# Attention with the two maps of a differential head merged into one output product, the values stationary and the probabilities moving

## The reference, cut to what matters

```python
def mix_groups(dq, dk, dv, gq, gk, gv, lam, lam_init, subln_g):
    sc = HEAD_DIM ** -0.5
    o1 = attend(dq[:, :, :, 0], dk[:, :, :, 0], dv, sc)      # 4 differential heads, map 1, values 128 wide
    o2 = attend(dq[:, :, :, 1], dk[:, :, :, 1], dv, sc)      # map 2, the same values
    o_diff = rmsnorm(o1 - lam.astype(o2.dtype) * o2, subln_g) * (1.0 - lam_init)
    o_gqa = attend(gq, gk, gv, sc)                           # 8 query heads, 2 key/value heads, values 64 wide
    return jnp.concatenate([o_diff.reshape(b, L, -1), o_gqa.reshape(b, L, -1)], axis=-1)
```

## Time and profile before

| what | value |
|---|---|
| median of 3 runs | 2672.94 us (2671.48 to 2678.66) |
| the profiled execution, first to last instruction | 2675.0 us, inside the range of the runs, 2.1 us above their median |
| TensorE busy | 2410.9 us, 90% |
| VectorE busy | 1675.5 us, 63% |
| ScalarE busy | 974.4 us, 36% |
| GpSimd busy | 591.1 us, 22% |
| attention: first DMA issue to VectorE's last operation | 469.8 to 1127.0 us |
| granted TensorE clock, mean | 0.956 of 2.4 GHz |

### The profile page before, as it was taken

One profiled execution on the slowest core, in us unless ns is written; L12 is line 12 of the kernel. 1 busy time (PEld: TensorE's weight loads), 2 busy tenths in 40 slices (PEclk: granted clock), 3 DMA queues, 4 the chain that ended last, 5 costly groups with the idle time before them and its releaser, 6 DMA issues. The chain is left out here.

```text
span 2675.0 us, 44908 instructions
## 1 busy us (share of the span) xinstructions
PE 2410.9 (90%) x11570; PEld 1565.9 (59%) x11571; DVE 1675.5 (63%) x3837; ACT 974.4 (36%) x1958; POOL 591.1 (22%) x393
## 2 busy tenths in 40 slices
PE   7699997699999999869993999999999999999993
PEld 2255553588999888734442555555555555555552
DVE  1213332577776777624444777777788787878886
ACT  0011111465666556511110334333333333333333
POOL 0000000300000000000001244444444344344444
PEclk9899998799999999989996999999999999999997
DMA  9701112500000000051103899878999967779955
GB/s 337 272 29 34 33 25 72 132 25 16 16 24 16 24 24 16 26 184 63 63 31 113 288 302 338 236 207 238 323 344 352 344 158 224 232 195 326 291 141 165
DMA packets 242105, 419.64 MB, mean 157 GB/s; under 512 B 11151, under 2 KB 181391, under 8 KB 241047
## 3 DMA queue, kind: packets, MB, share of 16 engines
q1 hardware_dynamic: 202048, 285.51, 31.1%
q0 software_dynamic: 33984, 123.75, 18.2%
q10 hardware_dynamic: 6044, 10.06, 1.0%
HBM read 338.88 MB, written 80.40 MB: 157 GB/s over the span
## 5 line engine op out<-in xcount | busy, mean ns | idle before, releaser
L1512 PE MATMUL ps_gu<-w_gate_up,gatheredT 128*128 x1680 | 747.8, 598 | 6.8 <-SPq L1320 6.8
L1512 PEld LDWEIGHTS ps_gu<-w_gate_up,gatheredT 128*128 128x128 f32 x1680 | 311.7, 190 | 365.4 <-issue 362.7
L1335 POOL DMA_INDIRECT gathered<-h_scratch,e_gather_index x107 | 303.0, 2832 | 65.8 <-issue 38.3
L1347 POOL DMA_INDIRECT y_scratch<-e_y,e_target_index x104 | 165.5, 1592 | 653.3 <-DVE e_y L1465 617.2
L828 PE MATMUL ps_out<-values,probsT 128*128 128x128 f32 (+1 forms) x2560 | 303.8, 274 | 0.0
L741 DVE TENSOR_REDUCE chunk_max<-ps_scores 128x1 f32<-128x512 f32 (+1 forms) x387 | 222.5, 599 | 126.5 <-PE ps_scores L813 109.2
L828 PEld LDWEIGHTS ps_out<-values,probsT 128*128 128x128 f32 x2560 | 296.7, 192 | 0.5
L1448 DVE TENSOR_TENSOR w_down_low<-w_down,w_down_high 128x2048 fp32r<-128x2048 f32 x105 | 240.7, 2292 | 81.6 <-issue 81.6
L529 PE MATMUL ps_chunk<-w_in_sb,hT 128*128 128x512 f32 (+1 forms) x736 | 286.0, 550 | 1.5 <-ACT hT L339 1.5
L704 ACT ACTIVATE probs<-ps_scores,neg_max 128x512 f32<-128x512 f32 (+1 forms) x387 | 233.7, 613 | 48.5 <-DVE neg_max L746 42.7
L1373 ACT ACTIVATE e_gate_a<-ps_gu 128x256 f32<-128x256 f32 x105 | 40.3, 384 | 543.1 <-PE ps_gu L1512 543.1
(11 more groups left out here) (229 smaller groups left out, 3067.2 us busy)
## 6 DMA issues: line engine op xcount, KB each, us to landing
w_gate_up<-in_w_exp_gate SPq DMA_DIRECT2D x64, 1024.0 KB
w_gate_up<-in_w_exp_up SPq DMA_DIRECT2D x64, 1024.0 KB
w_down<-in_w_exp_down SPq DMA_DIRECT2D x64, 1024.0 KB
w_mod_ring<-in_w_mod SPq DMA_DIRECT2D x24, 1024.0 KB, 11.6
w_in_sb<-in_w_in SPq DMA_DIRECT2D x8, 1152.0 KB, 12.6
q_twice<-qT_scratch SPq DMA_DIRECT2D x34, 256.0 KB, 4.0
x_tile<-in_tokens SPq DMA_DIRECT2D x10, 512.0 KB, 3.4
qT_scratch<-qT_stage SPq DMA_DIRECT2D x20, 256.0 KB, 3.6
```

The costliest lines, as they stand in the source:

```text
L1335: pool.indirect_dma_start(xg[u][:], None, h2_d, bass.IndirectOffsetOnAxis(ap=ti[u][:, 0:1], axis=0), bounds_check=SEQ - 1).then_inc(s_gath ...
L1347: pool.indirect_dma_start(y_d, bass.IndirectOffsetOnAxis(ap=si[u][:, 0:1], axis=0), yb[u][:], None, bounds_check=SEQ + P - 1, compute_op=A ...
L1512: last = nc.tensor.matmul(psG[:], hT[:, k], wgu[:, ds(q & (WS - 1), 1), k].rearrange("p o n -> p (o n)"), start=(k == 0), stop=(k == KD - 1))
```

## The change

Attention is written out anew, with no hardware loop. The work is cut into 24 units. A `d` unit is four query tiles (512 queries) of one differential head; there are 8, in two groups of four. A `g` unit is one query tile and the four query heads of one key/value head; there are 16, in two groups of eight. The order is 4 d, 8 g, 4 d, 8 g.

- Scores: one step makes two maps for 128 queries side by side in five PSUM banks (2560 columns; the third bank holds the end of the first and the start of the second): both maps of a differential head, or two query heads. A d unit has 4 steps, a g unit 2. Now the keys hold high and low in the two halves of one tile, and q is stationary as `qh` and then `ql`. Each is still two fp32r products. There is one set of score banks. The second map's columns in the last bank pair wait for both exponentials of the step before.
- Maxima: one reduce of 1280 columns, one of 256, one of 1024, and a minimum of two. Exponentials: two instructions of 1280 columns.
- Merge, d units only: VectorE makes minus lambda times the quotient of the two row sums; GpSimd multiplies the second map by it and adds the product to the first (1280 columns each).
- Transposes: for each of ten key blocks, four 128 x 128 blocks into one of two PSUM banks, 512 columns; ScalarE copies them out. In g units, where the product is made in fp32r, VectorE also writes the remainder (`low_p`), reading the same bank.
- Output product: the values of a key block are stationary (128 columns: a differential head's 128, or high and low of a 64 wide one), the 512 transposed probabilities move. d: float32. g: two fp32r products. The result is transposed: ScalarE copies it out, TensorE turns it back (`back`), VectorE scales it.
- Of the ten key heads ScalarE now takes all high parts and VectorE all low parts, two before the first scores, the others between the steps of units 0 and 1. Storing the results and all q loads are on SP's queue (q loads now move pieces of 128 elements, 512 bytes).
- The load of the four modulation rows moves from `projections` to the start of `output_and_router`, on SP's queue behind the first input tiles.

The diff, cut; its order is projections, output_and_router, then attention with tiles, SP, GpSimd, ScalarE, VectorE and TensorE:

```diff
-            spread(sp, mod_d, later_rows, [(0, 4), (0, 3), (0, 2), (0, 5)], s_rows2)
...
+            spread(sp, mod_d, rows, [(0, 4), (0, 3), (0, 2), (0, 5)], s_rows2)
...
+    QB = 4
+    KEEP = 4
+    units = []
+    for qb in range(SEQ // (QB * P)):
+        units += [("d", qb, p) for p in range(DH)]
+        units += [("g", qb * QB + t, h) for t in range(QB) for h in range(GKV)]
+    MID = {"d": {1: 1, 3: 2, 6: 3}, "g": {4: 1}}
...
+        pr = b.sb(ph, "probs", [P, 2, 4, KEYS])
+        pb = b.sb(ph, "probs_second", [P, 2, KEYS])
+        psS = b.pb(ph, "ps_scores", [P, 5, 512])
+        psT = b.pb(ph, "ps_probsT", [P, 2, 512])
+        psO = b.pb(ph, "ps_out", [P, 512])
...
+            for u in range(NU):
+                if 0 < u < NU - 2:
+                    load_q(u + 2)
+                if u >= 1:
+                    store(u - 1)
...
+            def mix(u, i):
+                s, n = first[u] + i, n_mix[u] + i
+                B = pb[:, s % 2]
+                A = pr[:, u % 2, i]
+                pool.wait_ge(s_c, n + 1)
+                nc.gpsimd.tensor_scalar(B, B, cs[:, n % 2, 1:2], None, ALU.mult).then_inc(s_cs, 1)
+                pool.wait_ge(s_cs, n + 1)
+                nc.gpsimd.tensor_tensor(A, A, B, ALU.add).then_inc(s_mix, 1)
...
+            for u in range(NU):
+                for kt in range(KT_N):
+                    out_p(u, kt)
+                    if kt == 0 and pend:
+                        exp_a(*pend[0])
+                    if kt == 1 and pend:
+                        exp_b(*pend[0])
+                        pend = []
+                    if kt == 4 and u + 2 < NU:
+                        q_high(u + 2)
+                    if kt >= 1 and kt - 1 in mid:
+                        exp_a(u + 1, mid[kt - 1])
+                    if kt >= 2 and kt - 2 in mid:
+                        exp_b(u + 1, mid[kt - 2])
+                    if late and kt in (2, 5):
+                        k_high(late.pop(0))
+                out_o(u)
...
+            for u in range(NU):
+                if u + 1 < NU:
+                    max_a(first[u + 1])
+                for kt in range(KT_N):
+                    if kt == 0 and u + 1 < NU:
+                        max_b(first[u + 1])
+                    low_p(u, kt)
+                    if kt == 1 and u >= 1:
+                        finish(u - 1)
+                    if kt == 2:
+                        if u + 1 < NU:
+                            second_scale(u + 1, 0)
+                        if late:
+                            k_low(late.pop(0))
+                    if kt == 5 and late:
+                        k_low(late.pop(0))
+                    if kt == 4 and u >= 1:
+                        finish_norm(u - 1)
+                    if kt == 5 and u + 2 < NU:
+                        q_low(u + 2)
+                    if kt in mid:
+                        max_a(first[u + 1] + mid[kt])
+                    if kt >= 1 and kt - 1 in mid:
+                        max_b(first[u + 1] + mid[kt - 1])
+                    if kt >= 3 and kt - 3 in mid:
+                        second_scale(u + 1, mid[kt - 3])
...
+            def qk(u, i):
+                s = first[u] + i
+                if s >= 1:
+                    pe.wait_ge(s_ea, s)
+                for row, at, key, w in ((0, 0, 0, 512), (0, 512, 512, 512), (0, 1024, 1024, 256), (1, 1280, 0, 256),
+                                        (1, 1536, 256, 512), (1, 2048, 768, 512)):
+                    if at == 1024 and s >= 1:
+                        pe.wait_ge(s_eb, s)
...
+            def tr(u, kt):
+                g = u * KT_N + kt
+                if g >= 2:
+                    v = (g - 2) // KT_N
+                    if units[v][0] == "g":
+                        pe.wait_ge(s_lo, n_low[v] + (g - 2) % KT_N + 1)
+                    else:
+                        pe.wait_ge(s_ev, g - 1)
+                for j in range(4):
+                    if kt == 0:
+                        if units[u][0] == "d":
+                            pe.wait_ge(s_mix, n_mix[u] + j + 1)
...
+            LAG = 3
+            for u in range(NU):
+                mid = MID[units[u + 1][0]] if u + 1 < NU else {}
+                for kt in range(KT_N):
+                    tr(u, kt)
+                    if kt == 1 and u >= 1:
+                        back(u - 1)
+                    if kt >= LAG:
+                        pv(u, kt - LAG)
+                    if kt in mid:
+                        qk(u + 1, mid[kt])
+                if u + 2 < NU:
+                    qk(u + 2, 0)
+                for kt in range(KT_N - LAG, KT_N):
+                    pv(u, kt)
+            back(NU - 1)
```

More of the change, by code:

```diff
@@ new lines, in attention, with n_steps @@
+    QB = 4
[4 more added lines that the diff above has]
+        units += [("g", qb * QB + t, h) for t in range(QB) for h in range(GKV)]
+    NU = len(units)
+    def n_steps(u):
+        return 4 if units[u][0] == "d" else 2
+    first = [sum(n_steps(v) for v in range(u)) for u in range(NU + 1)]
+    NS = first[NU]
+    n_low = [sum(KT_N for v in range(u) if units[v][0] == "g") for u in range(NU + 1)]
+    n_diff = [sum(1 for v in range(u) if units[v][0] == "d") for u in range(NU + 1)]
@@ new lines, in attention, with kv_head, q_cols, q_width @@
+    n_mix = [sum(4 for v in range(u) if units[v][0] == "d") for u in range(NU + 1)]
+    MID = {"d": {1: 1, 3: 2, 6: 3}, "g": {4: 1}}
+    def kv_head(u, row):
+        kind, _, p = units[u]
+        return 2 * p + row if kind == "d" else 2 * DH + p
+    def q_cols(u, i, row):
+        at = row * 512 + i * P if units[u][0] == "d" else (2 * i + row) * P
+        return slice(at, at + P)
+    def q_width(u):
+        return 1024 if units[u][0] == "d" else 512
+    def slots(u, i):
+        return (i, None) if units[u][0] == "d" else (2 * i, 2 * i + 1)
@@ L854, in output_and_router @@
-def output_and_router(b, a, ident, rows, s_rows2, mhalf, x1, entry, mask, before, part, count, o_d, h2_d, y_d):
+            def qk(u, i):
+                s = first[u] + i
+                if i == 0:
+                    pe.wait_ge(s_ql, u + 1)
+                pe.wait_ge(s_kl, kv_head(u, 1) + 1)
+                if s >= 1:
[4 more added lines that the diff above has]
+                        pe.wait_ge(s_eb, s)
+                    cols = q_cols(u, i, row)
+                    for part in (qh, ql):
+                        last = nc.tensor.matmul(S[:, at:at + w], part[:, u % 2, cols], k2[:, kv_head(u, row), key:key + w],
+                                                start=(part is qh), stop=(part is ql))
+                    if at == 1280:
+                        last.then_inc(s_sa, 1)
+                last.then_inc(s_sb, 1)
@@ new lines, in back @@
+            def back(u):
+                pe.wait_ge(s_oT, u + 1)
+                for j in range(4):
+                    if units[u][0] == "d":
+                        last = nc.tensor.transpose(psO[:, j * P:(j + 1) * P], oT[:, j * P:(j + 1) * P], ident[:])
+                    else:
+                        pe.wait_ge(s_id, 1)
+                        last = nc.tensor.matmul(psO[:, j * HD:(j + 1) * HD], oT[:, j * P:(j + 1) * P], id2[:], start=True, stop=True)
+                last.then_inc(s_ob, 1)
@@ L857, in output_and_router @@
+            back(NU - 1)
+def output_and_router(b, a, ident, rows, s_rows2, mod_d, mhalf, x1, entry, mask, before, part, count, o_d, h2_d, y_d):
     nc = b.nc
```

489 lines of the change are left out of this document (262 added, 227 removed).

## The result

The changed kernel takes 2710.34 us, the median of 4 runs (2707.97 to 2713.1); the kernel before took 2672.21 beside it. The ratio is 1.0138, 95% interval 1.0124 to 1.0152: slower by 38 us, where 20 us faster were forecast. The profiled execution has a span of 2706.2 us.

What follows compares the result with a forecast made beforehand. TensorE bounded attention before; afterwards, waits between nearly equally loaded engines would. Unit times summed to attention ending at 1103 (-24 us), moved rows added 4, net -20: 2653 us, range 2600 to 2705.

Steps and rivals of the forecast that it cites:

- The bound before: Attention in the old kernel: TensorE sets its time, busy 581.5 of 616 us; its work falls from 575 to 413.
- The other engines' durations: VectorE and ScalarE in attention: maximum 1.47 us at 1280 columns, 1.21 at 1024; exponential 1.31, copy 0.60, 512-column operation 0.69.
- A g unit followed by a g unit: Attention's g units: laid out wait by wait, 20.65 us each, where TensorE's work is 14.5 and VectorE's 15.1.
- Where the clock goes: TensorE in g units: thin stretches lower the clock, one loss of 1.65 us a unit, giving 22.3; bounds 20.65 and 28.1.
- Rival 2: G units so thin that TensorE is mostly at 1.2 GHz: 28.1 us each, kernel 2734 us; chance 0.25.
- A d unit followed by a d unit: Attention's d units: a chain through GpSimd's merges at 4.2 us each returns every 28.6 us, 29.5 with a hold.
- Rival 3: GpSimd's scalar product costs 2.91 us, a merge 5.8: kernel 2687, or 2670 to 2680 at half the excess; chance 0.1.
- GpSimd can also be held by VectorE: D units: VectorE's q low pass delays GpSimd's chain by 0 to 1.3 us, taken as 0.9.
- The advice that I set aside: Merges on VectorE in d units: its 20.5 us would become some 32 a unit, more than 29.5, so no gain.
- The start: Attention's beginning: first scores at 486, first transposes at 522; further key heads cost units 0 and 1 about 6 us.
- The moved rows: Modulation rows loaded at the output stage's start: 4 us taken, 0 to 5.4 possible; 0 in `projections`.
- The sum: Units from 522 total 581 us: attention ends at 1103 (-24), net -20 with the rows; profiled 2655, median 2653.

Runs made afterwards that it cites:

- The run with dead work: Kernel with the merge on VectorE, plus a GpSimd product and addition behind each merge on a tile nobody waits for: 2714.7 us, ratio 1.0154.

## Why the prediction was wrong

**The bound before.** TensorE's busy time in attention did fall (581.5 to 495 us), and attention didn't shorten by it, as forecast: other work became the length. That part stands.

**The other engines' durations** were right where the row was of the same kind: 1.49 for a maximum of 1280 (1.47 said), 1.215 for 1024 (1.21), 1.33 for an exponential (1.31), 0.69 for a remainder, 0.60 for a copy.

**A g unit followed by a g unit.** Laid out at 20.65, it takes 20.2, and 20.2 again and again. The layout by waits was sound; that TensorE's turns between transposes and products were left out of its 14.5 did not show, since TensorE waits there anyway. Without the remainder it is 17.9.

**Where the clock goes.** The 1.65 us a unit that I added for it were not there: the granted clock was 1.00 from 780 to 800 and 0.94 from 650 to 850. Rival 2 (28.1 us a g unit) fell with it. It had the right sign for the kernel, by another cause. Among d units the granted clock was lower, 0.88 from 870 to 1000; with the merge on VectorE the same units have 0.95 (840 to 950), and with no merge 1.00 (788 to 917). The forecast had a clock loss in the g units, which came out at their 20.2 us without it, and none in the d units, where the waits were longer and the clock lower. What the lower clock cost there no run takes out by itself.

**A d unit followed by a d unit: the step that failed.** It said "The product by a scalar has one tile input, so I take 1.25 (bounds 1.25 and 2.91), 4.2 a merge." It is 3.64 and 3.02, so 6.7 a merge. Rival 3 had named 5.8 at most, and 2687. The wrong was in the choice of the nearest row: a conversion and a product are both one-input passes of 1280 columns, and one is 2.9 times the other.

The path itself was laid out rightly: 16 us to the second scale, then three merges in a row, then the next unit's transposes. Measured from row to row in the second block it returns every 37.0, 38.6 and 38.1 us where 29.5 was said. The three merges take 20.2 to 20.6 us of it, where the forecast had 12.6, and 0.9 for a hold of GpSimd. That hold is there as forecast: q low starts first (885.27, 1.22 us), and the product behind it takes 4.42 in place of 3.52. The rest of the way takes 16.9 to 17.9 us for 16, with one held operation of line 846 in it (1.85 us each time). With the price alone put right in the forecast's own layout, 7.4 us more in each of seven chains, it gives an estimate of 52 us more: 2705 where 2710 was measured.

That sum is nearer than it should be. The first two chains of the first block have no such row: GpSimd waits 3 to 8 us before three of their four merges. They take 46 us each for 32.5, with the key splits, held operations and a lower clock among them, and their excess wasn't taken apart.

What the forecast missed beside the price is the other direction of "GpSimd can also be held by VectorE". Rows 9 and 10 showed a small operation of GpSimd waiting for a VectorE pass with two inputs; I took it as a price GpSimd pays. GpSimd's passes are the long ones here, so VectorE's small operations wait up to 2.2 us. The run with dead work shows that this costs 54 us where nobody waits for GpSimd, so the merge's 79 us can't be split into 54 of hold and 25 of waiting for the result. The two overlap: where three merges stand in a row, GpSimd is the later one and the holds beside the row are hidden behind it. Whether the holds would set the unit with a faster product was not tried; no run takes the two apart with GpSimd's result in use.

The Trainium skill states the rule behind the holds ("SBUF — State Buffer", SBUF: two separate sides): GpSimd and VectorE share a pair of ports under an exclusive lock; a VectorE operation with two inputs in SBUF and a GpSimd operation that reads SBUF exclude each other for a whole instruction. The trace agrees in each kind: lines 846 and 857 and the low parts of q (up to 3.95 us for 1.22) and of the keys (up to 3.53 for 1.49), with two inputs in SBUF, are held; the maxima, the reciprocal and the remainder (one of its inputs is in PSUM; 689 ns here and with GpSimd idle) are not. For how long isn't settled: to the end of the addition, but 0.45 us less than the product's.

**The advice that I set aside.** On the rule of the Trainium skill ("GPSIMD Engine Reference", Engine selection) that elementwise work belongs on VectorE I concluded that "by this rule followed the sum would not be lower", since VectorE's 20.5 us a unit would become 32. The run with the merge on VectorE says 2660.4 against 2710.3, so the rule holds here and the conclusion was wrong. The merge is 1.55 us there, so 4 x 1.55 = 6 us a unit, not 11.5; I had counted two passes with their waits where one instruction does it. The d units of the second block then took 28.2 on average (112.7 for four, the last ahead of a g unit), where the forecast, with GpSimd, was 27.1 and the changed kernel 34.8. The same section of the Trainium skill has one-input work on GpSimd at about VectorE's rate. The conversion agrees (1.25 us, where VectorE's low part of a key head, also 1280 columns, is 1.49); the product doesn't: it takes 3.5 us where VectorE's product and addition together take 1.55, and the measurement decides.

**The start.** First transposes were to come at 522; three of the four query tiles were, from 521.75 on, and the last merge held the fourth to 530.02. The first scores came at 485.3 (486 said).

**The moved rows.** 4 us said, bounds 0 and 5.4; 7 measured, outside the bounds, and 2.7 net, as shown above. The bound failed because it counted only the rows' own bytes. In `projections` nothing moved, as said.

**The sum.** Against the forecast: d units +75 with the start, g units -17, and behind attention -7 (1545.1 us for 1548.0, where +4 was said; +2.7 is the stage's start, -5.6 lies in later stages whose code is the same, and wasn't followed up). That is +51 between the profiled executions (2706 for 2655), and the medians stand 57 apart, 2710.3 for 2653, since this time the profiled execution is the fastest of the four. What stays open, beside this, is how price, holds and clock share the excess of the first block's d units, and why the product beside VectorE costs 14 us more than its holds.

## What to carry to other kernels

Take an unknown duration from a row of the same operation, since one of the same shape alone was off by a factor of 2.9; if there is no such row, let the upper bound go beyond the dearest row at hand. Before work goes to an idle GpSimd, look for VectorE operations with two operands in SBUF on the path, however small: each may wait for the GpSimd instruction beside it. Dead work shows what a hold can cost, not what it costs where something else is late too. Where several engines have nearly the same work, lay a unit out wait by wait: that came within 0.5 us of 20.2, where the engine sums were 14.5 and 15.1.

## What the runs showed of the hardware

- GpSimd over 128x1280 float32: a conversion 1.25 us, an addition of two tiles 2.91, a product by a scalar 3.52, by a constant 3.45 (the medians of their lines; the means are above). The one-input product is dearer than the two-input addition.
- Beside it, a VectorE operation of one column with two inputs in SBUF took up to 2.02 us in place of 0.16 (line 846); operations with one input in SBUF, or with one of two in PSUM, kept their time. Where VectorE's operation started first, GpSimd's product took 4.42 us in place of 3.52.
- TensorE, turning between four transposes and a 512-column float32 product, took 0.15 us a turn more than inside rows of the same kind.
- Four loads of 512 KB on SP's queue beside ScalarE's weight loads delayed TensorE's start by 7 us, through longer issue instructions on ScalarE's queue, though at the 405 GB/s that the DMA engines moved from 1170 to 1175 their bytes are 5.2 us.
